# HGRN scores on the diagonal: a product of keys and queries on VectorE, summed by TensorE with a matrix of ones, in place of eight 128x128 products

## The reference

```python
cum = jnp.cumsum(gi, axis=2)
diff = cum[:, :, :, None, :] - cum[:, :, None, :, :]
decay = jnp.exp(jnp.where(causal[:, :, None], diff, -jnp.inf))
scores = jnp.einsum('bhtk,bhtsk,bhsk->bhts', qi, decay, ki)
```

## Time and profile before

| What | Value |
|---|---|
| median of three runs | 2290.14 us (2290.10 to 2290.18) |
| the profiled execution | 2290.84 us |
| its span in the profile | 2289.0 us |
| granted TensorE clock, mean | 0.998 of full speed |
| busy share PE, DVE, ACT, POOL | 99%, 70%, 36%, 49% |

### The profile page before, as it was taken

How to read it: one execution, slowest core, us unless ns; L and a number is a source line. 1 busy time by engine, 2 the same in 40 slices (tenths; PEclk the granted TensorE clock), 3 DMA queues, 4 the chain that set the end, 5 groups by cost and what they waited for, 6 DMA issues and landing times.

```text
span 2289.0 us, 32255 instructions
## 1 busy us (share of the span) xinstructions
PE 2269.7 (99%) x10808; PEld 1895.1 (83%) x10808; DVE 1601.1 (70%) x2259; ACT 817.2 (36%) x1332; POOL 1111.6 (49%) x1256
## 2 busy tenths in 40 slices
PE   9999999999999999999999999999999999999998
PEld 7888888888888888888888888888888888888886
DVE  7666666756778777876656666555687877787766
ACT  5233333324544434444430002002453444344432
POOL 4332323244666566655543334444556665666561
PEclk9999999999999999999999999999999999999999
DMA  4111010124264556455312111111235545554553
GB/s 156 37 30 36 29 37 28 38 74 147 92 212 147 176 181 211 146 177 181 120 46 83 37 38 39 45 47 47 101 138 184 187 147 197 183 187 146 199 194 138
DMA packets 56966, 265.40 MB, mean 116 GB/s; under 512 B 6960, under 2 KB 8112, under 8 KB 39472
## 3 DMA queue, kind: packets, MB, share of 16 engines
q1 hardware_dynamic: 55872, 262.10, 33.5%
q10 hardware_dynamic: 1008, 2.15, 0.3%
HBM read 206.55 MB, written 57.67 MB: 115 GB/s over the span
## 4 chain that ended last, share of the span: by engine, by line
PE 93%; DVE 3%; DVEq 1%; ACT 1%; issue 0%; SPq 0%; DMA 0%; ACTq 0%
PE prod_ps L754 13%; PE prod_ps L756 12%; PE prod_ps L755 12%; PE prod_ps L1010 8%; PE prod_ps L1011 8%; PE prod_ps L1012 8%; PE side_ps L1010 7%; PE side_ps L1011 7%; PE side_ps L1012 7%; PE side_ps L895 2%; PE side_ps L807 2%; PE side_ps L813 1%; PE side_ps L823 1%; PE side_ps L825 1%; PE side_ps L833 1%; PE prod_ps L1044 1%
## 5 line engine op out<-in xcount | busy, mean ns | idle before, releaser
L754 PE MATMUL prod_ps<-operand_hi,w_hi 128*128 128x512 f32 x1336 | 532.8, 399 | 2.8 <-DVE operand_lo L1444 2.6
L756 PE MATMUL prod_ps<-operand_hi,w_lo 128*128 128x512 f32 x1336 | 522.2, 391 | 0.0
L755 PE MATMUL prod_ps<-operand_lo,w_hi 128*128 128x512 f32 x1336 | 520.8, 390 | 0.0
L578 POOL CAST w_hi<-w_raw 128x1024 fp32r<-128x1024 f32 x81 | 86.7, 1070 | 656.6 <-PE prod_ps L756 632.3
L582 POOL TENSOR_TENSOR w_lo<-w_raw,w_hi 128x256 fp32r<-128x256 f32 x324 | 303.5, 968 | 6.5
L754 PEld LDWEIGHTS prod_ps<-operand_hi,w_hi 128*128 128x128 f32 x1336 | 251.4, 188 | 55.5 <-DVE operand_lo L1444 3.2
L756 PEld LDWEIGHTS prod_ps<-operand_hi,w_lo 128*128 128x128 f32 x1336 | 251.0, 188 | 54.0
L755 PEld LDWEIGHTS prod_ps<-operand_lo,w_hi 128*128 128x128 f32 x1336 | 251.6, 188 | 48.8
L623 POOL TENSOR_TENSOR w_lo<-w_raw,w_hi 128x256 fp32r<-128x256 f32 x168 | 155.2, 944 | 128.9 <-ACT w_hi L2541 128.4
L623 POOL TENSOR_TENSOR w_lo<-w_s,w_hi 128x256 fp32r<-128x256 f32 x168 | 129.5, 774 | 142.0 <-ACT w_more_hi L2549 115.8
L1855 DVE TENSOR_TENSOR x_res<-prod_ps,x_res 128x512 f32<-128x512 f32 x130 | 89.0, 685 | 95.5 <-PE prod_ps L1012 95.4
(11 more groups left out here) (366 smaller groups left out, 5411.2 us busy)
## 6 DMA issues: line engine op xcount, KB each, us to landing
w_raw<-stream SPq DMA_DIRECT2D x202, 512.0 KB, 3.7
x_park<-x_res SPq DMA_DIRECT2D x45, 1024.0 KB, 8.2
x_res<-x_park SPq DMA_DIRECT2D x45, 1024.0 KB, 6.8
swapped<-op_park SPq DMA_DIRECT2D x39, 1024.0 KB, 5.0
op_park<-swapped SPq DMA_DIRECT2D x6, 1024.0 KB, 7.4
x_in<-x_t SPq DMA_DIRECT2D x16, 256.0 KB, 5.7
x_res<-x_t SPq DMA_DIRECT2D x8, 512.0 KB, 4.5
out_t<-x_res SPq DMA_DIRECT2D x16, 256.0 KB, 2.1
```

The costliest lines, as they stand in the source:

```text
L578: nc.gpsimd.tensor_copy(w_hi[:, slot], w_raw[:, slot]).then_inc(high_made, 1)
L754: nc.tensor.matmul(into, w_h, a_h, start=(k == 0), stop=False)
L755: nc.tensor.matmul(into, w_h, a_l, start=False, stop=False)
L756: last = nc.tensor.matmul(into, w_l, a_h, start=False, stop=(k == KT - 1))
```

## The change

L0 is no longer made of keys by queries on TensorE. VectorE multiplies keys and queries of the same token, element by element, half by half (`h_diag`, right behind each of the two products of q with its sigmoid). ScalarE copies the two halves with rounding to fp32r (`h_diag_hi`), at the end of its iteration. VectorE subtracts and so makes the low part (`h_diag_lo`, 128x1024, in the place of `h_diag`), as the first instruction of the next iteration. TensorE then sums over the partitions: a matrix of ones by the high part and by the low part, two halves each, four matmuls of 128x512 in fp32r, at the place where the eight products were. Every row of the result holds the same sums, and VectorE's product with the identity picks the diagonal as before. TensorE's wait at L0 is now for the low part (`diag_ready`). The matrix of ones is written once at the start. The rest is as it was.

```diff
                 def level(number, h, b):
                     if number == 0:
-                        pe.wait_ge(qk_ready, h + 1)
+                        pe.wait_ge(diag_ready, h + 1)
                         pair = pair_free(step("L0"))
-                        blocks_128(pair, lambda c: h_block(b, False, c), lambda c: h_block(b, True, c))
+                        for half in range(NH):
+                            tok = slice(half * HALF, (half + 1) * HALF)
+                            nc.tensor.matmul(side_ps[:, pair, tok], all_ones[:], h_diag_hi[:, tok], start=True, stop=False)
+                            mm = nc.tensor.matmul(side_ps[:, pair, tok], all_ones[:], h_diag_lo[:, tok],
+                                                  start=False, stop=True)
+                        mm.then_inc(side_done, 1)
                         return
...
+            nc.vector.memset(all_ones[:].bitcast(F32), 1.0)
...
+                def diagonal_low():
+                    if newer:
+                        dve.wait_ge(diag_high, n * 2)
+                        nc.vector.tensor_tensor(h_diag_lo[:], h_diag[:], h_diag_hi[:].bitcast(F32), ALU.subtract
+                                                ).then_inc(diag_ready, 1)
...
                     elif j >= 4:
                         dve.wait_ge(q_sig, n * 2 + (j - 3))
                         q = h_part(par, True, j - 4)
-                        last = nc.vector.tensor_tensor(q, q, by_chunk(sig[:, j - 4]), ALU.mult)
+                        nc.vector.tensor_tensor(q, q, by_chunk(sig[:, j - 4]), ALU.mult)
+                        dve.drain()
+                        if static and n == 0 and j == 4:
+                            pass
+                        elif j == 4:
+                            dve.wait_ge(side_done, step_number(hgrn_step(n, "L0", i, par)) + 1)
+                        nc.vector.tensor_tensor(by_chunk(h_diag[:, tokens(j - 4)]), h_part(par, False, j - 4), q, ALU.mult
+                                                ).then_inc(diag_made, 1)
                         if j == 5:
-                            last.then_inc(qk_ready, 1)
-                            dve.drain()
+                            dve.sem_inc(qk_ready, 1)
...
+                diagonal_low()
                 if older:
                     level(par, LEVELS - 1)
                 newer_level(0)
...
+                def diagonal_high(half):
+                    act.wait_ge(diag_made, n * 2 + half + 1)
+                    nc.scalar.activation(h_diag_hi[:, tokens(half)], h_diag[:, tokens(half)], ACT.Copy
+                                         ).then_inc(diag_high, 1)
...
                 q_sigmoid(1)
+                diagonal_high(0)
+                diagonal_high(1)
```

More of the change, by code:

```diff
@@ L246, in h_block @@
             return h_kq[b][:, (c + query) % 2, c * BLK:(c + 1) * BLK]
+        h_diag = place("hgrn_diag", [P, S], at=at_r0 + 72 * KB)
+        h_diag_lo = place("hgrn_diag_lo", [P, S], F32R, at=at_r0 + 72 * KB)
+        h_diag_hi = place("hgrn_diag_hi", [P, S], F32R, at=at_r0 + 76 * KB)
+        all_ones = place("all_ones", [P, P], F32R)
         def by_chunk(x):
@@ L378, in build @@
         qk_ready = sem("qk_ready")
+        diag_made = sem("diag_made")
+        diag_high = sem("diag_high")
+        diag_ready = sem("diag_ready")
         level_mixed = sem("level_mixed")
```

## The result

The changed kernel takes 2295.24 us (median of 19 runs, 2292.46 to 2297.18), the kernel before 2290.34 (19 runs, 2289.36 to 2291.15). The ratio is 1.0021, with a 95% interval from 1.0015 to 1.0027: slower by 4.9 us. The profiled execution of the changed kernel took 2294.62 us with a span of 2292.8, that is 3.8 above the one of before.

The account below looks back on a forecast made before the run. TensorE was taken to bound the kernel, filling the whole HGRN iteration. Waits 11.6 plus reloading 0.7 less a gain of 6.9 gave +5.4 us, 2295.5 on the median; 8-in-10 range 2291.0 to 2299.5.

Parts of the forecast that it names:

- TensorE's gain, 0.86 a head and 6.9 in all: At L0, four 128x512 matmuls replace eight 128x128 products, saving 0.86 us a head, 6.9 us for eight heads.
- The chain in front of L0: Four more dependent steps on VectorE and ScalarE before L0, at least 3.5 us later, against head 7's slack of 2.7.
- The waits, 11.6: TensorE's added waits at L0: 4.1 at head 0, 4.0 at heads 4, 5, 7, 3.5 at the other four.
- Three heads (4, 5, 7) have this pattern: Head 7's step-by-step chain, with GpSimd stretching VectorE, gives a 1.34 us wait at L0; 4.0 us for the three heads.
- The four heads put at 0.9: L0 of heads 1, 2, 3 and 6: 0.9 us of waiting taken for each, 3.5 us together; head 1 worked out at 0.85.
- The clock, left out of the sum as a rival at 0.16: Behind head 0's wait TensorE's clock falls, 1.6 us lost, making the sum +7.0, 2297.1 us; chance 0.16.
- Reloading, 0.7: After a wait at L0 TensorE loads weights otherwise loaded beside other work: 0.1 us for seven new waits, 0.7.
- Head 0, 4.1: L0 of head 0 has no slack; its subtraction, behind `load_masks`, ends at 55.9, so L0 starts 4.1 us later.
- The turning of k: Twelve large matmuls behind L0, at 390.8; VectorE finishes L7's mask by 389.3, so it doesn't wait.
- VectorE's delay: About 3 us of lateness on VectorE, gone before L1, ahead of which it sat idle for 4.15 us.
- a gain of 4 to 6.9 us: Rival: L0's operand comes within 0.25 us of its place, so TensorE is never kept waiting much; chance 0.09.

Follow-up runs that it names:

- the run of that part alone: Changed kernel with the four matmuls by ones on zero-filled buffers, without the new VectorE and ScalarE steps: 2282.35 us, ratio 0.9964 to the kernel before.
- the runs with v first: ScalarE copies turned v ahead of both rounding copies: with only the new VectorE and ScalarE steps and the eight old products, 2290.31 us; in the changed kernel, 2294.50.
- e8_all_three: Changed kernel with the shorter chain, head 0's L0 moved into the next large product, and v copied ahead of the second rounding copy: 2282.55 us.
- the one with the shorter chain: Changed kernel with the diagonal's first half behind the last scaled copy and the subtraction in halves at the same iteration's end: 2286.45 us.
- the one with the new order alone: Changed kernel with the diagonal's first half behind the scaled copy of the last product, subtraction whole and in its place: 2291.83 us.

## Why the prediction was right, and where it was not

*TensorE's gain, 0.86 a head and 6.9 in all:* right, by the run of that part alone.

*The chain in front of L0:* right in kind. Every L0 waited, every wait was released by the subtraction, the diagonal's first half took 1.07 or more at every head, and the steps have the lengths that were put in: 0.69 to 1.37, 0.68, 0.63, 0.69 to 1.24, 0.63, 1.23. Shortening the chain, with all of the work left in, brought heads 1 to 7 from 4.6 us of waiting to 0.7 and head 0 from 4.07 to 2.2.

*The waits, 11.6:* 8.4, too large by 3.2: 1.6 of it at heads 4, 5 and 7, 1.3 at heads 1, 2, 3 and 6, and 0.4 at head 0. This is the term that was mis-sized, and the step behind it is "Three heads (4, 5, 7) have this pattern". The pattern was read off one execution. There the 16-column product of VectorE, 0.1 us behind GpSimd's copy, was held for 1.05 us at those three heads (at 232.06, 280.73 and 378.05; the last in the earlier trace rows), and everything behind it ran 0.9 later. In the changed kernel's trace it was held at head 5 alone, and at head 7 it passed, though it came as close behind:

```profile
284.70 1.10 POOL L586 CAST w_hi<-w_raw 128x1024 fp32r<-128x1024 f32 x1 [13.12 <-PE prod_ps L764]
284.78 1.05 DVE L1560 TENSOR_TENSOR hgrn_decay<-hgrn_decay 128x16 f32<-128x16 f32 x1
...
382.33 1.16 POOL L586 CAST w_hi<-w_raw 128x1024 fp32r<-128x1024 f32 x1 [13.12 <-PE prod_ps L764]
382.42 0.17 DVE L1560 TENSOR_TENSOR hgrn_decay<-hgrn_decay 128x16 f32<-128x16 f32 x1
```

The trace of the kernel before could have warned: at head 6 the product passed, with the copy's start as close ahead of it.

```profile
329.30 1.16 POOL L578 CAST w_hi<-w_raw 128x1024 fp32r<-128x1024 f32 x1 [13.12 <-PE prod_ps L756]
329.39 0.16 DVE L1546 TENSOR_TENSOR hgrn_decay<-hgrn_decay 128x16 f32<-128x16 f32 x1
```

Head 5 waited 1.21 us at L0, head 7 0.56. In the runs with v first and with the wait filled, the hold and the wait of over 1 us were at head 4; in the run with L0 of head 0 later neither was at any of heads 1 to 7. It is a race between two engines for one turn, worth 0.6 us a time, and a trace shows only how it went once. Where it was held, the forecast was near (1.21 for 1.34). The four heads put at 0.9 (1, 2, 3 and 6; only head 1's rows were worked through) waited 0.86, 0.38, 0.38 and 0.64: head 1's price was not that of the others.

*The clock, left out of the sum as a rival at 0.16:* it fell, and cost 1.7, the price that the rival had (1.6). What was held against it, that TensorE was saturated before and behind the wait, didn't keep the clock up; with the wait filled it held. The rule of the Trainium skill (TensorE: Matmul & The Clock Gate, Part 1), that idleness takes the clock down, deserved the larger chance; the trace agrees with it, with 0.57 behind the wait.

*Reloading, 0.7:* 0.8, that is 0.09 to 0.12 at each of seven heads. *Head 0, 4.1:* 3.74 added, with the masks 0.5 of it. *The turning of k* didn't wait, and VectorE's delay was gone before L1 of head 7, as put: it still sat idle for 3.3 us ahead of it. One slip stands in the rivals: a gain of 4 to 6.9 us is a time of 2283.2 to 2286.1, not "2284 to 2286"; nothing hangs on it.

The sum as it was: 8.4 waits, 0.8 reloading, 1.7 clock, less 6.9: +4.0, where the traces, from ahead of head 0's L0 to behind head 7's, differ by 3.8. The forecast had 12.3 - 6.9. So the mechanism was right and the number owes part of its closeness to luck: 3.2 us too much of waiting and 1.7 too little of clock met halfway, and the medians' 4.9 then lie nearer to 5.4 than the profiled executions' 3.8, which is chance.

What stays open: why the 19 runs of the changed kernel spread over 4.7 us, where the five of `e8_all_three` spread over 0.7 and the 19 of the kernel before over 1.8. The race and how much of the clock's fall lies in the wait could do it, but that is not shown: each kernel has one trace. For the same reason the 1.7 us of the clock are a price of single executions (head 0's fall cost 1.7 in the changed kernel and in the one with the shorter chain, and more in the one with the new order alone).

## What to carry to other kernels

Work moved off a saturated engine gains only what the moved work's own chain leaves: measure the slack between the operand's readiness and its use, and add up the dependent steps across engines, not the load of each. When the slack is short, don't give up the cheaper form; put independent halves under waits that exist already, split the last step, and move the use behind work that doesn't need it. Look at every semaphore of the waiting instruction and at what a new step displaces in the other engines' queues.

## What the runs showed of the hardware

A wait of 3.9 us on a TensorE that had been saturated for 25 us was followed by the lower clock (0.57 over 56 to 60), and so was one of 2.1 us in the run with the shorter chain (0.76 and 0.81 over 52 to 60), at the same cost of 1.7 us; one of 1.2 us was not (1.00 in the run with head 0's L0 later). Sixteen matmuls whose result is overwritten kept it at 2.4 GHz.

A VectorE product of two SBUF operands and 128x512 took 0.69 us by itself and 1.07 to 1.37 beside GpSimd's weight splitting. The Trainium skill (SBUF — State Buffer, "SBUF: two separate sides") has this as a lock for whole instructions; the trace agrees, with 1.05 us for 16 columns at head 5 beside a copy of 1.10. At head 7 the same product took 0.17 and the copy 1.16. In both rows the copy starts 0.08 to 0.09 us ahead, so which of the two gets its turn first can't be read from their starts.
